# The experts of a streaming encoder layer as two loops over their blocks, with four 32 KB weight slots and another order of transfers

## The reference

```
h   = x + mixer(rmsnorm(x))
xf  = rmsnorm(h) * norm_ffn
group = argmax(xf @ w_router_group + b)                 # 4 groups
top 2 of 8 experts inside the group, gates from two softmaxes
for each expert e of 32:                                # its tokens
    hb = silu(xb @ w_gate[e]) * (xb @ w_up[e])          # 2048 -> 512
    out += (hb @ w_down[e]) * gate                      # 512 -> 2048
y = rmsnorm(h + out) * norm_final
```

## Time and profile before

| | us |
|---|---|
| median of 3 runs | 1521.53 |
| lowest and highest | 1520.55, 1521.89 |
| the profiled execution | 1520.34 |
| its span | 1518.4 |
| around the span | 1.9 |
| PE busy | 1343.2 |
| DVE busy | 590.5 |
| ACT busy | 347.6 |
| bytes read from HBM | 469.97 MB |

### The profile page before, as it was taken

The page is one execution under the profiler, slowest core; times in us unless marked ns, Lnnn a source line. Parts: engine busy times, 40 slices in busy tenths (PEclk is TensorE's granted clock), DMA queues, the critical chain, the costliest instruction groups (busy, mean ns, idle before and its releaser), DMA issues.

```text
span 1518.4 us, 22122 instructions
## 1 busy us (share of the span) xinstructions
PE 1343.2 (88%) x8510; PEld 714.2 (47%) x8511; DVE 590.5 (39%) x1175; ACT 347.6 (23%) x595; POOL 32.4 (2%) x41
## 2 busy tenths in 40 slices
PE   6999999999999999787888888888889988888885
PEld 4989999566666663232222222322323322232221
DVE  4335444044574443242243234224324422332344
ACT  5332322123453322111111111111212111111113
POOL 1000000000000000000000000000000000000000
PEclk9999999999999989999898888988989989898887
DMA  9454451023353368999999999999989999999994
GB/s 324 131 166 137 161 167 61 10 70 111 92 180 112 131 285 355 408 432 430 432 433 432 429 433 433 431 429 433 433 369 400 432 434 432 428 434 432 432 428 180
DMA packets 69751, 473.91 MB, mean 312 GB/s; under 512 B 9532, under 2 KB 46656, under 8 KB 55824
## 3 DMA queue, kind: packets, MB, share of 16 engines
q1 hardware_dynamic: 68640, 470.78, 76.0%
q0 software_dynamic: 832, 2.48, 0.4%
q10 hardware_dynamic: 240, 0.09, 0.0%
HBM read 469.97 MB, written 3.38 MB: 312 GB/s over the span
## 4 chain that ended last, share of the span: by engine, by line
PE 52%; DMA 41%; DVE 3%; issue 2%; ACT 1%; DVEq 0%; SPq 0%; ACTq 0%
DMA ring<-in_w_down 41%; PE ps L888 11%; PE ps L587 5%; PE ps L588 5%; PE ps L589 5%; PE ps L873 3%; PE ps L649 2%; PE ps L676 2%; PE ps L739 2%; PE ps L740 2%; PE ps L741 2%; PE ps L752 2%; PE ps L850 2%; PE ps L670 1%; PE ps L879 1%
## 5 line engine op out<-in xcount | busy, mean ns | idle before, releaser
L1566 DVE TENSOR_TENSOR hreg<-ps,hreg 128x512 f32<-128x512 f32 (+1 forms) x396 | 239.4, 677 | 291.6 <-PE ps L899 291.6
L873 PE MATMUL ps<-ring,mix 128*32 128x512 f32 x2112 | 278.4, 675 | 31.7 <-DMA ring<-in_w_up 19.5
L888 PE MATMUL ps<-ring,mix 128*32 128x512 f32 x1056 | 165.7, 784 | 62.5 <-DMA ring<-in_w_down 54.7
L899 PE MATMUL ps<-mix 32*128 32x512 f32 (+1 forms) x792 | 156.3, 612 | 26.4 <-ACT mix L1249 25.6
L1206 ACT COPY mix<-ps 128x512 f32<-128x512 f32 x66 | 70.5, 1068 | 446.4 <-PE ps L873 446.4
L873 PEld LDWEIGHTS ps<-ring,mix 128*32 128x32 f32 x2112 | 74.5, 121 | 206.3 <-issue 176.2
L587 PE MATMUL ps<-xT_hi,w_hi 128*128 128x320 f32 (+1 forms) x528 | 165.6, 314 | 2.9 <-DVE w_lo L1301 2.9
L588 PE MATMUL ps<-xT_lo,w_hi 128*128 128x320 f32 (+1 forms) x528 | 164.6, 312 | 0.0
L589 PE MATMUL ps<-xT_hi,w_lo 128*128 128x320 f32 (+1 forms) x528 | 164.5, 312 | 0.0
L1301 DVE TENSOR_TENSOR w_lo<-ring,w_hi 128x1024 fp32r<-128x1024 f32 (+1 forms) x66 | 76.8, 1204 | 110.5 <-ACT w_hi L1019 110.5
L888 PEld LDWEIGHTS ps<-ring,mix 128*32 128x32 f32 x1056 | 39.6, 138 | 162.7 <-issue 104.4
(11 more groups left out here) (258 smaller groups left out, 1186.5 us busy)
## 6 DMA issues: line engine op xcount, KB each, us to landing
ring<-in_w_gate SPq DMA_DIRECT2D x31, 4096.0 KB, 22.2
ring<-in_w_up SPq DMA_DIRECT2D x31, 4096.0 KB, 23.7
ring<-in_w_down SPq DMA_DIRECT2D x31, 4096.0 KB, 23.7
ring<-in_w_in SPq DMA_DIRECT2D x32, 1024.0 KB, 8.2
ring<-in_w_o SPq DMA_DIRECT2D x16, 1024.0 KB, 6.7
ring<-in_w_up SPq DMA_DIRECT2D x2, 2048.0 KB, 11.7
ring<-in_w_gate SPq DMA_DIRECT2D x2, 2048.0 KB, 8.4
ring<-in_w_down SPq DMA_DIRECT2D x2, 2048.0 KB, 22.3
```

The source lines that it names most:

```text
L873: last = pe.matmul(ps[r:r + B, bank, :], x[:, k % 4, k // 4, :], w[:, k, :], start=k < 4, stop=k >= KC - 4)
L888: last = pe.matmul(ps[B * j:B * (j + 1), 4, :], h[:, c, :], w[:, c, 512 * j:512 * j + 512], start=c == 0, stop=c == 3)
L899: pe.matmul(ps[0:tn, COMB_BANKS[u % 8], :], gates[r, t0:t0 + tn], rows[r, :], start=True, stop=True).then_inc(full_sem, 1)
L1566: dve.tensor_tensor(h, ps[0:tn, COMB_BANKS[u % 8], :], h, ALU.add).then_inc(signal, 1)
```

## The change

Four things change, and what hangs on them.

*Slots and order of transfers.* A fourth buffer `gate_b` of 32 KB per partition lies over `mix`, `ckv` and the head of `cq`. Even experts take their gate matrix from the ring, odd ones from `gate_b`. SP loads the gate matrix of expert 1 as soon as `hg_ready` reaches 12, before the tables are there. In its loop it issues for each e: the gate of e+1, the up of e, the down of e. Only for the last two experts the order is again up 30, down 30, gate 31, up 31, and down 31 goes in four transfers of 1 MB, with `down` waiting for each piece.

*Two loops per expert.* There is no separate code for an extra block. A first loop over the expert's blocks does gate, gather, fold, transposes, up and fold, and writes silu times up of each block to its place in `hTs`; a second loop does `gates_T`, down and combine for each block, with ACT first copying the block's part of `hTs` to `hT`. PE has the code of an expert twice (even and odd).

*Order inside a block.* `gathered_T` stands ahead of the up matmuls; `copy_xT` stands ahead of the up half's `copy_half` on ACT; `gates_T` stands after the wait for `hT_ready`; the banks of `combine` go in another order and the next gate waits for 7 adds instead of 6.

*Loads around it.* The router's weights move to `krt` and `const`, and their loads behind the loads of x; DVE scales `wr` in the second quarter of the output projection instead of before the first; PE waits for it accordingly. The final gain is loaded into the gate slot of the ring when the last piece of down 31 has landed. A few small DVE operations of the routing go or come.

```diff
-COMB_BANKS = (5, 6, 7, 1, 4, 2, 0, 3)
+COMB_BANKS = (5, 6, 7, 1, 0, 4, 2, 3)
...
-        wr = cq[:, :, :].rearrange("p c t -> p (c t)")[:, 0:KC * 36]...
+        wr = krt[:, 0:KC * 36].rearrange("p (c e) -> p c e", c=KC)
...
+        gate_b = nc.alloc_sbuf_tensor_at("gate_b", [P, 2 * SLOT], F32, offset=mix_at)
...
             sp.wait_ge(psum_full, full(f"K{H - 1}_1"))
+            sp.dma_start(gain, a["norm_ffn"].to_broadcast([P, D])).then_inc(s_gffn, 16)
+            sp.wait_ge(psum_full, full(f"PV{H - 1}"))
...
+            for i, (t0, tn) in enumerate(TILES):
+                sp.dma_start(xtile[0:tn, i, :], x_src[i]).then_inc(s_xagain, 16)
             sp.dma_start(wr[:, :, 0:G], ...)          # the four router loads
...
-            sp.wait_ge(routed, 4)
-            with sp.Fori(1, NE) as e:
-                ...  gate e, up e, down e
+            sp.wait_ge(hg_ready, 12)
+            sp.dma_start(gate_b[:, :], rows_of(0, a["w_gate"][0, 1])).then_inc(gate_b_full, 16)
+            sp.wait_ge(routed, 2)
...
+            with sp.Fori(1, NE - 3, 2) as e:
+                before = blocks_before(e)
+                load_gate(e + 1, before, gate_a, slot_full[0])
+                load_up(e, before)
+                load_down(e, before)
+                before = blocks_before(e + 1)
+                load_gate(e + 2, before, gate_b[:, :], gate_b_full)
+                load_up(e + 1, before)
+                load_down(e + 1, before)
...
+            sp.wait_ge(down_done, before)
+            for c in range(4):
+                sp.dma_start(ring[:, 4 + c // 2, D * (c % 2):D * (c % 2 + 1)],
+                             rows_of(2, a["w_down"][0, NE - 1])[:, D * c:D * (c + 1)])...
...
-            pool.wait_ge(hg_ready, 12)
-            pool.dma_start(gain, a["norm_final"]...
+            pool.wait_ge(down_last[2], 17)
+            pool.dma_start(gain_last, a["norm_final"]...
...
+            def expert(e, odd):                                        # PE
+                first = pe.value_load(tables[0:1, 0, bass.ds(e, 1)], ...)
+                count = pe.value_load(tables[0:1, 1, bass.ds(e, 1)], ...)
+                with pe.Fori(0, count) as k:
+                    it = first + k
+                    pe.wait_ge(xg_ready, it + 1)
+                    pe.wait_ge(comb_added, first * 12 + 7)
+                    gate_full(e, odd)
+                    gate_or_up(xg, 0, odd, 2).then_inc(gate_done, 1)
+                    pe.wait_ge(comb_added, first * 12 + 8)
+                    pe.wait_ge(pick_ready, it + 2)
+                    gather(pickr, 0, gathered)
+                    pe.wait_ge(h_copied, it * 2 + 1)
+                    pe.wait_ge(hT_ready, it + 1)
+                    fold(0).then_inc(folded, 1)
+                    pe.wait_ge(g_copied, it + 2)
+                    pe.wait_ge(comb_added, first * 12 + 12)
+                    gathered_T(gsb, 1, transposed)
+                    matrix_full(1, e)
+                    gate_or_up(xg, 1, odd, 4).then_inc(up_done, 1)
+                    pe.wait_ge(h_copied, it * 2 + 2)
+                    pe.wait_ge(silu_ready, it + 1)
+                    fold(1).then_inc(folded, 1)
+                tail = pe.value_load(tables[0:1, 2, bass.ds(e, 1)], min_val=0, max_val=16)
+                after = first + count
+                with pe.Fori(0, count) as k:
+                    it = first + k
+                    pe.wait_ge(hT_ready, after + 1)
+                    pe.wait_ge(comb_added, it * 12 + 5)
+                    pe.wait_ge(gates_ready, it + 1)
+                    gates_T(gpick, gt_full)
+                    pe.wait_ge(comb_added, it * 12 + 6)
+                    pe.wait_ge(h_picked, it + 1)
+                    down(hT, e, tail + 1).then_inc(down_done, 1)
+                    pe.wait_ge(xg_ready, after + 1)
+                    pe.wait_ge(gt_copied, it + 1)
+                    pe.wait_ge(y_copied, it + 1)
+                    pe.wait_ge(comb_added, it * 12 + 12)
+                    combine(gT, yb, comb_full, comb_added, it * 12 + 12)
...
+                    act.wait_ge(up_done, it + 1)                       # ACT, first loop
+                    copy_xT(xg, 1, transposed, it + 2, xg_ready)
+                    copy_half(1, 4, h_copied)
...
+                    act.wait_ge(hT_ready, after + 1)                   # ACT, second loop
+                    act.copy(hT, hTs[:, bass.ds(k, 1), :]...).then_inc(h_picked, 1)
+                    act.wait_ge(gt_full, it + 1)
+                    act.copy(gT, ps[:, 0, 0:T]).then_inc(gt_copied, 1)
+                    act.wait_ge(down_done, it + 1)
+                    act.copy(yb, ps[:, 4, :]).then_inc(y_copied, 1)
```

More of the change, by code:

```diff
@@ L255, in trunk_layer_kernel @@
         gate = work[:, w0 + 252:w0 + 258].rearrange("p (i k) -> p i k", i=3)
-        dest, rank, high, place, placex = (
-            work[:, w0 + 258 + 6 * k:w0 + 264 + 6 * k].rearrange("p (i k) -> p i k", i=3) for k in range(5))
+        rank, place, shift = (work[:, w0 + 258 + 6 * k:w0 + 264 + 6 * k].rearrange("p (i k) -> p i k", i=3) for k in range(3))
         w0 += 288
@@ L974, in _ @@
+            for c in range(3):
+                pe.sem_inc(down_last[c], 1)
             keep_clock(3, 5)
@@ L978, in _ @@
             gathered_T(gsb, 1, transposed)
-            pe.wait_ge(routed, 4)
-            expert(0, slice(0, 1), True)
-            with pe.Fori(1, NE) as e:
-                expert(e, bass.ds(e, 1), False)
+            pe.wait_ge(routed, 2)
+            with pe.Fori(0, NE - 1, 2) as e:
+                expert(e, False)
+                expert(e + 1, True)
         @block.scalar
```

358 lines of the change are left out of this document (136 added, 222 removed).

## The result

The changed kernel takes 1528.58 us (median of 12 runs, 1521.86 to 1534.07), the kernel before 1520.63 us beside it (12 runs, 1517.83 to 1524.25): a ratio of 1.0049, 95% interval 1.0037 to 1.0060. Run again on another chip it took 1525.96 us (6 runs), a ratio of 1.0050, 1.0033 to 1.0068. It is slower by 7 to 8 us where I had forecast 11 faster. The sign was wrong, and the time lies outside the range of 1504.5 to 1520.

The account below looks back on a forecast made before the run. It took the stream of weight transfers, 9.71 us each, to bound the expert stage. Terms -9.7 - 1 + 0.6 - 1.2 = -11.3 gave span 1507.1 and median 1510.2 us, range 1504.5 to 1520.

Parts of the forecast that it names:

- What bounds it before: Expert stage: a stream of transfers at 432 GB/s, 9.71 us per 4 MB; PE counts only where it makes holes.
- The early gate and the start of the loop: Expert 1's gate loaded in the hole before gate 0, -9.7 us; first-pass pause gone from loop start, -1 (-3 to +3).
- rival 1: Stream starts late: gate 0 or the first pass waits 3 to 6.5 us for code; 1515.5 us, chance 0.17.
- The end: After the last landing: four-piece `down` has a quarter of its matmuls left, PE about ready; -1.2 us (-3.5 to +2).
- The round of PE: PE's work per expert: grows 2.6 to 25.9 us, about 30 with two slow groups, against 29.14; nothing for the sum.
- The expert with two blocks: Queue holes about that expert: 2.1 to 3.8, 5.4 and 0.3 us, say 8.6 against 8 before; +0.6 (-3.5 to +5).
- my slow case: Two-block expert with a slow first gate: 16.1 us from gate to second fold's end, second gate used at 31.5.
- The router's loads and the final gain: Loads behind x have 7 and 4 us cover, at worst +2; gain lands in the tail, at worst +1; nothing expected.
- Rival 3: PE becomes the bound: loops, reads and branches add over 3.2 us to every round; about 1526 or 1610, chance 0.13.

Follow-up runs that it names:

- One block each: Both kernels with the second block of the two-block expert left out: before 1513.20 us (0.9955), changed 1512.00 us (0.9942).
- order undone: Changed kernel with `gathered_T` back behind the up, `copy_half` ahead of `copy_xT`, `gates_T` ahead of the `hT_ready` wait: 1519.01 us, 0.9984.
- reads and gate moved: Changed kernel with in-block order undone, PE table reads moved, and next gate behind up and down from expert 15 on: 1509.45 us, 0.9928.

## Why the prediction was wrong, step by step

The sum was -11.3; the measured change is +7 to +8.

**What bounds it before**: right. Up to the two-block expert and behind it the queue runs at 432 GB/s in the changed kernel too, and taking the early gate back costs 7 us.

**The early gate and the start of the loop**, -9.7 and -1: right, the second on the low side. One block each, gate 0 to the last landing fell by 13.2 us where these had 10.7. Gate 0 itself comes 1.0 us later, with two table reads now ahead of it, where I had nothing. No pause of 3 to 6.5 us stood there or in the first pass, so rival 1 was false, though its sign (gate 0 later than 571) shows in the first profile.

**The end**, -1.2: this step failed, and it turned the sign. I took PE to be ready 1.6 us ahead of the last landing, as in the earlier trace rows, less what a round grows. The earlier trace rows show a PE that has 29.14 us for every round. The change's own text has up 30 and down 30 issued ahead of gate 31, so the last two rounds have 48.6 us together, where PE takes 56.8. I had counted the transfers to the last landing and not those between two downs. With my own round of 25.9 the lag would have been 3.2 us, with the real one it is 8.2; the tail grew by 8.2 and 9.6 us in the two profiles. The order of the queue alone, moved in one run, takes it away.

**The round of PE**, "nothing for the sum": failed with it. 25.9 was right for a round in which all matmul groups take 3.64 us: the round from 1400.54 to 1427.99 took 27.45, of which its `down` had 5.14 and its gate 3.73, so 25.9 without. But most rounds have a slow group. I expected fewer as PE idled less. There were as many: 10 of the 11 downs between 1172.67 and 1484.97 us (8 of 12 from 1170 us on in the kernel before). The windows show what the form is:

```profile
1472.91:1478.25 5.34, 5.33 (x33) 1.28 (x32) 1.69 (x5) 0.42 (x1) 0.00 (x0) 0.68 0.93 399
1503.27:1506.91 3.64, 3.64 (x33) 0.94 (x32) 1.67 (x5) 0.42 (x1) 0.00 (x0) 1.00 0.00 0
1484.97:1491.50 6.53, 6.53 (x36) 1.68 (x40) 2.58 (x5) 0.00 (x0) 0.00 (x0) 0.55 0.92 386
```

The same 32 matmuls take 3.64 us at a granted clock of 1.00 (2.4 GHz), 5.34 at 0.68 and 6.5 at 0.55, which is most of the group at 1.2 GHz. PE had been busy 3.67 of the 6 us ahead of the `down` that fell (from 1467 on) and 2.84 of the 5.2 ahead of the one that didn't (from 1498 on), so these rows give no simple sign of which will fall. A round is 25.9 plus 1.7 to 2.9 for each fallen group, and I had no ground to expect fewer of them.

**The expert with two blocks**, +0.6: failed, by 6 to 9 us. Counted from the down matrix at 1106.6, the first gate came at +13.0 where I had +11.8, the second gate was used up at +33.8 where I had 29.8 to 31.5, both downs at +58.9 where I had 54.6 to 56.3. SP's issues in the changed kernel:

```profile
1140.50 0.34 SPq L480 DMA_DIRECT2D gate_b<-in_w_gate  x1
1148.10 0.33 SPq L484 DMA_DIRECT2D ring<-in_w_up  x1
1165.51 0.33 SPq L488 DMA_DIRECT2D ring<-in_w_down  x1
1178.22 0.34 SPq L480 DMA_DIRECT2D ring<-in_w_gate  x1
```

The queue had run dry at 1106.6 + 29.1 = 1135.7, so the first hole is 6.2 us with 1.4 from issue to flow, against my 2.1 to 3.8; the second is 5.6 against 5.4. The last line is a hole that I had at 0.3: the down issued at 1165.51 was through at 1176.6, and the next gate of the queue comes 1.6 later plus 1.4, when the slow gate of the next expert (1172.67, 5.34 us) has used its slot. Together 14.8 us against 8.6; the windows have 17.2 in this profile and 14.6 in the second. The first hole's excess is mostly the slow form once more: the `down` ahead took 6.25 us where I had 5.3, the first gate 6.58 where my slow case had 5.34, together 2.2 of the 2.3 us by which the second gate missed my upper bound. The transposes were in my terms. With the order undone alone the empty part stayed at 15.2 us, and with reads and gate moved as well it was 10.7; how much each gave isn't shown.

**The router's loads and the final gain**, nothing: right. The gain landed 4.8 us after its issue and DVE's first scaling came at 1516.15, long behind.

**The rivals.** Rival 3, PE becomes the bound, had the sign and, by luck, about the size, 1526; its mechanism was another: it asked for rounds over 29.14 everywhere. The rounds are 28.4, below the point, and mid-stage nothing is lost. What I lacked was the same rival with the point moved to 24.3 us, half of five transfers, for two rounds at the end. On the rule that I weighed there (the Trainium skill, Runtime: NRT & Kernel Launch, Instruction fetch mechanics: a taken branch outside the window of fetched code waits for a fetch): this trace doesn't bear it out for every back-edge. It has three packets of instructions on the queue of the earlier trace rows in the whole of 575 to 630 us and none from 640 to 1500. The gates behind the outer loop's jump wait 1.58 us where the others wait 1.08, so a back-edge of this long body costs about half a us.

## What to carry to other kernels

When a prefetch takes a transfer out of a stream, ask behind which transfer each consumer gets its data early: with "next gate first" the gain arrives only in the last rounds, all at once, and there the compute engine's round, not the queue's, decides. A lead is cheap to place: put the tight pair of rounds where many later rounds can win the lag back, and the same instructions end 9 us sooner. And of two things that run side by side, a sequencer's reads and another engine's adds, the later is worth only its lead over the earlier, and the earlier nothing, until both are shortened.

## What the runs showed of the hardware that I had not expected

- The changed kernel spreads more than the one before, 1521.9 to 1534.1 us against 1517.8 to 1524.3, with the same program. In its 12 runs the mean granted clock falls as the time rises, from 0.941 in the fastest to 0.930 in the slowest. A matmul group at the lower clock takes 1.7 to 2.9 us more; where PE is the bound at the end this should lengthen the time, and where the stream is it can vanish in waits. The versions in which PE is in time spread by 5 us (1506.6 to 1511.9 and 1506.8 to 1512.2) and by 8 (1507.6 to 1516.0, ten runs), so that this makes the difference in spread is argued, not shown.
- The two bounds side by side ahead of a gate: 1.08, 0.80, 1.07 and 0.21 us of wait with neither, the one, the other and both taken away.
- ACT reloaded its tables twice in every block of the changed kernel, 66 times at 1.28 us, where the kernel before has no such load in its loop. One small silu ahead of the loop takes them away (440.9 to 357.9 us busy).
